# A decode row's share of a projection moved to four column groups of TensorE, and products of paged keys and queries moved from VectorE to GpSimd

## The reference, cut to what matters

```
h = rmsnorm(x)                                   # 1024 prompt rows, 8 sample rows, 1024 wide
sq, sk, sv, dq, dk, dv, ga, gb = split(h @ w_in) # first 3840 columns here, the gates later
dq, dk = rope(rmsnorm(dq)), rope(rmsnorm(dk))    # per head of 64
past = pool[page_table]                          # (8, 2048, 2, 8, 64), keys and values
z = einsum('bqhd,bkhd->bhqk', sq, past_keys) * 64 ** -0.5 + bias
```

## Time and profile before

| | us |
|---|---|
| median of 3 runs | 2374.56 |
| lowest, highest | 2369.94, 2378.31 |
| profiled execution | 2363.81 |
| its span, first to last instruction | 2362.0 |
| mean granted clock of TensorE | 0.949 of full speed |

### The profile page before, as it was taken

One profiled execution on the slowest core, in us unless ns is written; L12 is line 12 of the kernel. 1 busy time (PEld: TensorE's weight loads), 2 busy tenths in 40 slices (PEclk: granted clock), 3 DMA queues, 4 the chain that ended last, 5 costly groups with the idle time before them and its releaser, 6 DMA issues. The chain is left out here.

```text
span 2362.0 us, 38212 instructions
## 1 busy us (share of the span) xinstructions
PE 2154.9 (91%) x13126; PEld 1577.2 (67%) x13126; DVE 1416.2 (60%) x2146; ACT 1037.4 (44%) x1563; POOL 1022.6 (43%) x799
## 2 busy tenths in 40 slices
PE   7999799879699979999899979999999999999994
PEld 5777677667444438888777636776776677677663
DVE  4487678767576762111357527677667667766762
ACT  6221122245366652111234105666666566666662
POOL 2111222122366650011006603677677777767662
PEclk9999899957799999999999899999999999999997
DMA  6587701064445529893352059999999999999995
GB/s 219 171 271 246 225 32 38 28 190 124 161 135 155 169 82 299 263 302 112 110 190 91 23 194 319 332 323 318 326 329 318 323 329 321 323 325 326 319 320 136
DMA packets 180335, 520.57 MB, mean 220 GB/s; under 512 B 22908, under 2 KB 78867, under 8 KB 153791
## 3 DMA queue, kind: packets, MB, share of 16 engines
q1 hardware_dynamic: 133654, 366.37, 45.3%
q0 software_dynamic: 36208, 93.16, 15.6%
q10 hardware_dynamic: 10368, 59.73, 7.6%
HBM read 442.31 MB, written 125.08 MB: 240 GB/s over the span
## 5 line engine op out<-in xcount | busy, mean ns | idle before, releaser
L2474 DVE TENSOR_TENSOR w_gu_lo<-w_e,w_gu_hi 128x2048 fp32r<-128x2048 f32 x132 | 301.9, 2287 | 38.0 <-ACT w_gu_hi L2400 38.0
L2400 ACT ACTIVATE w_gu_hi<-w_e 128x2048 fp32r<-128x2048 f32 x132 | 253.5, 1920 | 44.4 <-DMA w_e<-in_w_e_gate 42.1
L565 PE MATMUL pP<-wring,hT_hi 128*128 128x512 f32 (+2 forms) x576 | 228.0, 396 | 21.8 <-DVE wring L500 12.7
L2336 PE MATMUL pG_e<-w_gu_hi,xT_hi 128*128 128x512 f32 x528 | 232.7, 441 | 1.0 <-issue 1.0
L567 PE MATMUL pP<-wring,hT_lo 128*128 128x512 f32 (+2 forms) x576 | 222.5, 386 | 0.0
L566 PE MATMUL pP<-wring,hT_hi 128*128 128x512 f32 (+2 forms) x576 | 222.3, 386 | 0.0
L2336 PE MATMUL pG_e<-w_gu_hi,xT_lo 128*128 128x512 f32 x528 | 208.9, 396 | 0.0
L2336 PE MATMUL pG_e<-w_gu_lo,xT_hi 128*128 128x512 f32 x528 | 208.1, 394 | 0.0
L2269 POOL DMA_INDIRECT x_scratch<-y_e,target x66 | 107.6, 1631 | 187.8 <-ACT y_tail L2438 187.8
L2255 POOL DMA_INDIRECT rows_tail<-h_scratch,index x66 | 176.5, 2675 | 20.8 <-issue 20.8
L429 ACT ACTIVATE stage<-pP 128x512 f32<-128x512 f32 (+3 forms) x72 | 41.1, 570 | 307.5 <-PE pP L567 303.5
(11 more groups left out here) (312 smaller groups left out, 5148.7 us busy)
## 6 DMA issues: line engine op xcount, KB each, us to landing
w_e<-in_w_e_gate SPq DMA_DIRECT2D x66, 1024.0 KB, 7.2
w_e<-in_w_e_up SPq DMA_DIRECT2D x66, 1024.0 KB, 11.5
w_e<-in_w_e_down SPq DMA_DIRECT2D x66, 1024.0 KB, 7.0
turned<-in_cache_sb_kv SPq DMA_DIRECT2D x256, 256.0 KB, 3.1
out<-in_cache_win_kv ACTq DMA_DIRECT2D x8, 4094.0 KB
turned<-in_w_in ACTq DMA_DIRECT2D x56, 256.0 KB, 6.2
turned<-in_w_in SPq DMA_DIRECT2D x16, 512.0 KB, 9.0
out<-in_cache_win_kv ACTq DMA_DIRECT2D x8, 1022.0 KB
```

The source lines that it names most:

```text
L565: pe.matmul(pP[:m, i % 4, :w], hi, w_hi(u), start=(c == 0), stop=False)
L2336: last = pe.matmul(pG[:, :, :], xs[:, r, c, :], ws[:, r, :, c, :], start=(n == 0), stop=(n == 3 * KC - 1))
L2400: act.activation(ghi[:, r, k, :, :].rearrange("p c f -> p (c f)"), w[:, r, k, :], ACT.Copy).then_inc(ghi_ready, 1)
L2474: dve.tensor_tensor(glo[:, r, k, :, :].rearrange("p c f -> p (c f)"), w[:, r, k, :], ghi[:, r, k, :, :].rearrange("p c f -> p (c f)").bitc ...
```

## The change

The first group keeps its order. In each later group the decode item comes first, at place 0, and the eight prompt tiles follow at places 1 to 8. For groups 1 to 7 the decode item is made in another way: eight float32 matmuls from the raw weights, not split, with the activations of the 8 decode rows padded to 32 columns with zeros. Chunk c goes to column group c % 4 of TensorE, that is to PSUM rows 32q to 32q + 31 (decode_parts). ScalarE copies these 128 rows to SBUF, and one more matmul with a 0/1 mask adds the four parts (decode_fold); TensorE issues it inside the next item, ahead of its third chunk. ScalarE's copy of the decode item waits for it in its place in the order. ScalarE also waits for decode_parts before it loads the next group's raw weights.

The products of keys and queries move from VectorE (score_keys) to GpSimd (weigh_keys), with their waits, at the same items; in GpSimd's program they stand behind the weight subtractions of place 8 and ahead of the item's square. VectorE keeps the reductions.

The additions to setup are three buffers, five semaphores, a zeroing on GpSimd, one copy on ScalarE of the decode rows' activations, and the mask, made by VectorE from the identity.

```diff
-        for t in range(NT):
+        for t in (range(NT) if not items else (NT - 1, *range(NT - 1))):
...
             def _(pool):
                 pool.memset(eps[:, :], EPS).then_inc(eps_set, 1)
+                pool.memset(hT_dec[:, :, :], 0.0).then_inc(dec_zero, 1)
...
+                def weigh_keys(n):
+                    s, c = divmod(n, NPC)
+                    if c == 0:
+                        pool.wait_ge(q_in[s % 2], 16 * (s // 2 + 1))
+                    pool.wait_ge(k_in[n % NKB], 16 * GP * (n // NKB + 1))
+                    if n:
+                        pool.wait_ge(s_score_ready, n)
+                    pool.tensor_tensor(prod, kbuf[:, n % NKB], q[:, s % 2, :].unsqueeze(1).broadcast_to([P, GP, SBW]),
+                                       ALU.mult).then_inc(s_prod_ready, 1)
...
                     if k < NK - 1 and t == NT - 1:
                         for c in range(POOL_LOW):
                             low_w((k + 1) * KC + c)
+                    if i in CHUNK_AT:
+                        weigh_keys(CHUNK_AT[i])
...
                     act.wait_ge(raw_ready, t + 1)
+                    if t == NT - 1:
+                        act.wait_ge(dec_zero, 1)
+                        act.activation(hT_dec[:, :, :NS], rawT(t), ACT.Copy).then_inc(dec_raw_ready, 1)
...
                         if t == 1:
+                            if k:
+                                act.wait_ge(dec_done, k)
                             for c in range(KC):
                                 load_w((k + 1) * KC + c)
...
                         m, w = rows_of(items[i]["t"]), items[i]["w"]
+                        if m == NS and k:
+                            act.wait_ge(dec_done, k)
+                            act.activation(dec_part[:, :w], pP[:, i % 4, :w], ACT.Copy).then_inc(dec_part_ready, 1)
                         act.wait_ge(p_ready, i + 1)
...
                 def score_keys(n):
                     s, c = divmod(n, NPC)
-                    if c == 0:
-                        dve.wait_ge(q_in[s % 2], 16 * (s // 2 + 1))
-                    dve.wait_ge(k_in[n % NKB], 16 * GP * (n // NKB + 1))
-                    if n:
-                        dve.wait_ge(s_score_ready, n)
-                    dve.tensor_tensor(prod, kbuf[:, n % NKB], q[:, s % 2, :].unsqueeze(1).broadcast_to([P, GP, SBW]),
-                                      ALU.mult).then_inc(s_prod_ready, 1)
                     dve.wait_ge(s_prod_ready, n + 1)
...
+                dve.wait_ge(ident_in, 16)
+                chain(dve.tensor_tensor(fold[:, :], ident[:, 0:NS], ident[:, 32:32 + NS], ALU.add))
+                chain(dve.tensor_tensor(fold[:, :], fold[:, :], ident[:, 64:64 + NS], ALU.add))
+                dve.tensor_tensor(fold[:, :], fold[:, :], ident[:, 96:96 + NS], ALU.add).then_inc(fold_ready, 1)
...
+                def decode_parts(i):
+
+                    k, w = i // NT, items[i]["w"]
+                    if k == 1:
+                        pe.wait_ge(dec_raw_ready, 1)
+                    pe.wait_ge(stage_ready, i - 3)
+                    for c in range(KC):
+                        q = c % QT
+                        pe.wait_ge(w_in[c], 16 * (k + 1))
+                        last = pe.matmul(pP[32 * q:32 * q + 32, i % 4, :w], hT_dec[:, c, :], w_raw(k * KC + c),
+                                         start=(c < QT), stop=(c >= KC - QT))
+                    last.then_inc(dec_done, 1)
+
+                def decode_fold(i):
+
+                    k, w = i // NT, items[i]["w"]
+                    if k == 1:
+                        pe.wait_ge(fold_ready, 1)
+                    pe.wait_ge(dec_part_ready, k)
+                    pe.matmul(pP[:NS, i % 4, :w], fold[:, :], dec_part[:, :w], start=True, stop=True).then_inc(p_ready, 1)
+
                 for i in range(NI + 2):
-                    if i < NI:
+                    if NT <= i < NI and i % NT == 0:
+                        decode_parts(i)
+                    elif i < NI:
...
                         for c in range(KC):
                             u = i // NT * KC + c
+                            if i > NT and i % NT == 1 and c == 2:
+                                decode_fold(i - 1)
...
-                            elif t == NT - 1:
+                            elif i % NT == NT - 1:
                                 last.then_inc(w_used, 1)
```

More of the change, by code:

```diff
@@ L166, in phase_project @@
         wraw = turned[:, 16:, :].rearrange("p a (b n) -> p (a b) n", n=512)
+        hT_dec = sb("hT_decode", [P, KC, P // QT])
+        dec_part = sb("decode_part", [P, 512])
+        fold = sb("decode_fold", [P, NS])
         stage = sb("stage", [P, NSTAGE, 512])
@@ L202, in phase_project @@
         p_ready = sem("p_ready")
+        dec_zero = sem("dec_zero")
+        dec_raw_ready = sem("dec_raw_ready")
+        dec_done = sem("dec_done")
+        dec_part_ready = sem("dec_part_ready")
+        fold_ready = sem("dec_fold_ready")
         stage_ready = sem("stage_ready")
@@ L349, in _ @@
                             low_w((k + 1) * KC + c)
+                    if i in CHUNK_AT:
+                        weigh_keys(CHUNK_AT[i])
                     if not items[i]["normed"]:
                         continue
-                    m = rows_of(t)
+                    m = rows_of(items[i]["t"])
                     pool.wait_ge(stage_ready, i + 1)
```

## The result

| | before | after |
|---|---|---|
| median, four runs each | 2373.05 | 2418.16 |
| lowest, highest | 2369.94, 2378.31 | 2416.91, 2428.60 |
| profiled execution's span | 2362.0 | 2415.3 |
| end of the projection in it | 473.5 | 520.1 |

The account below looks back on a forecast made before the run. The projection was taken as in balance: TensorE 6.0 us an item, VectorE's chunk 4.6, GpSimd mostly idle. Delay 45.5 plus 5.4 in groups 6 and 7 gave 51 us on a median of 2374.6: 2425, range 2392 to 2452.

Parts of the forecast that it names:

- product on GpSimd: One 128x2048 product of keys and queries, extrapolated from rows of smaller additions and a product: 4.5 us.
- end of product 31: Last GpSimd product in the projection, after 31 steps from a first product at 95.34: ends at 330.9.
- delay there: Lateness when group 5's decode item and one full item are done, 344.6 against 299.1 before: 45.5 us.
- The chain: Projection: GpSimd's product and VectorE's reduction take turns on one buffer, 7.0 us a chunk against 6.0 for TensorE's item.
- Rivals 1, 2 and 3: GpSimd product at 3.3 us (2387, chance 0.07), 5.7 (2464, 0.08), or below 2.9 (2362, 0.07).
- Rival 4: Decode matmuls' column groups don't overlap: 2 us more each item, 0 to 4 in all, 2427; inside the forecast's 0.78.
- The burst: GpSimd's five weight subtractions between two products at a group's end: 8.4 us, 5.6 at half width.
- The last item at the lower clock: Group 5's first full item: last four of eight chunks after the fifth subtraction at 1.2 GHz, 5.3 us.
- The decode item: Groups 1 to 7: 1.6 us where 5.6 stood, saving 4.0 in a full-width group, 2.0 in group 4.
- Rival 3: Product below 2.9 us, so the chain stays under TensorE and saved rows show: 13 us faster, 2362; chance 0.07.
- Groups 6 and 7: Short item under norm 7, norm 8's root held behind the fold: 62.5 against 59.8, +2.7 us at each boundary, 5.4.
- Neither is on the path: SyncE's key loads (keys 7.5 us after product n-2) and ScalarE's stage copies (slack of six items) are not late first.

Follow-up runs that it names:

- e2: Kernel before the change with only the products moved to GpSimd, decode rows as before: median 2423.1 us, ratio 1.0216 to the kernel before.
- e1: Changed kernel with the products of keys and queries back on VectorE, all else as changed: median 2370.8 us, ratio 0.9987 to the kernel before.
- e3: Changed kernel with each GpSimd product, and its reduction, made in two halves of 1024 elements: median 2403.8 us, ratio 1.0131 to the kernel before.
- e7: e1 with the fold issued ahead of norm 7's transposes in groups 6 and 7: median 2361.7 us, ratio 0.9966 to the kernel before.
- e6: e5 with all stores but the last of each prompt item in groups 3 and 4 issued by ScalarE: median 2356.3 us, ratio 0.9942.
- e5: e4 with group 6's weights loaded at place 2 of group 5, not place 1: median 2359.8 us, ratio 0.9962 to the kernel before.
- e4: Changed kernel with products on VectorE and the new decode form and order in groups 1 to 5 only: median 2360.1 us, ratio 0.9951.

## Why the prediction was right

Every step of its chain can be laid beside the rows. The mechanism came as forecast; the 4.4 us by which the forecast is too high at the projection's end are a sum of errors in both directions.

| step | forecast | measured |
|---|---|---|
| product on GpSimd | 4.5 | 4.58 (32 of them) |
| product to product | 7.0 | 7.1 |
| burst of subtractions | 8.4; 5.6 at half width | 7.54; 3.64 |
| end of product 31 | 330.9 | 329.6 |
| first full item of group 5 done | 344.6 | 340.6 |
| delay there | 45.5 | 41.5 |
| groups 6 and 7, excess over before | 2.7 each | 3.1 and 2.7 |
| end of the projection | 51 later | 46.6 later |
| median | 2425 | 2418.2 |

- **The chain** carried the argument, and the runs show it from both sides. With the products alone the loss is whole (e2), without them it is gone (e1), and with the turns broken up it shrinks to the next bound (e3). The extrapolation from rows of 256 to 768 elements to one of 2048 was right to 2%. Rivals 1, 2 and 3 fall with it: none of their prices for a product was met. Rival 4 falls too, by the decode item's row in e1: eight matmuls that did not overlap would take some 8 us at the fold's price, and took 1.92.
- **The burst** was too dear by 0.9 us each, by 2.0 at half width. The rows that I took had a product of VectorE take turns with each (3.42 us at 133.15 and 2.80 at 235.87, where it takes 2.29 alone). With the products away only VectorE's subtractions do, and at half width they began when the burst was nearly over (286.66, its end at 288.02). e1 has it the other way: with products on VectorE and the decode item short, the burst takes 10.4 us at 125.05. A duration from a contended row should have been cleaned of the contention that the change removes.
- **The last item at the lower clock** was too dear as well. I let four chunks of matmuls follow the last subtraction at half speed. TensorE had started on the first chunks at 330.94, right behind the first subtraction, and was back at full clock within the third chunk, so that the last four took 2.8 us and not 5.3. The four bursts were 4.5 us too dear in all and the end of the item behind the fifth subtraction 1.8, and the first product began 1.7 before 95.34. Against that, 32 products gave back 2.6 and the gaps between them 1.6. But for rounding that makes the 4.0 us by which the delay fell short: part of the closeness is luck, errors that cancel.
- **The decode item** was mis-sized: 2.9 us and not 1.6. I counted the records of the earlier trace rows as matmuls, and a float32 matmul leaves two. The item saves 2.7 us and not 4.0; over groups 1 to 5 that would be 12 us and not 18. That it did no harm to the forecast is luck of its place: in groups 2 to 5 it falls in the wait. Rival 3's price of 13 us was too good for the same reason, and would be 7.
- **Groups 6 and 7**: the root held behind the fold was expected 16.8 us after place 8's end and came at 16.3. e7 took the cause away and the time came back.
- **"Neither is on the path"** was true of SyncE and the key buffers only under a chain of 7 us, and even there not quite: the product at 303.97 waited 4.02 us for keys where a turn costs 2.46, because SyncE's issue stood behind a late item's stores, an order that the prediction named and then gave no price. Once the chain is gone they are next, at 6.5 us a chunk with GpSimd (e3), and with VectorE through the issues of SyncE (e6) and the weights that share the transfers (e5). That is one reason why e1 gave 6 us at the projection's end where 11 were expected; the decode item's size is the other. With 12 us from the item, less the 3.0 that e1 lost in groups 6 and 7, 9 us were to be had, and 3 are left for the keys, as far as one profile tells. My first expectation asked what TensorE saved and not what would then be last.

## What to carry to other kernels

An idle engine is not free capacity when its work and another engine's share one buffer: price the round trip (here 4.6 + 2.3 + 0.2 us against 6.0 of cover), and not the busy shares. A saving on the engine that sets the pace shows only up to the next limit, so follow the queue that feeds it, issue by issue, before counting the gain. And where an engine runs in order, a short item's copy that waits for a late one (the fold) holds everything written behind it.

## What the runs showed of the hardware

- Eight float32 matmuls of 32 by 512, over four column groups, took 1.92 us at full clock and 3.64 at the lower one; the fold of 8 by 512 took 1.02 and 1.87. Eight stand in the trace as 16 records and one as two.
- GpSimd's two-input float32 operations: 1024 elements 2.39 us, 2048 elements 4.58, also when VectorE's one-input sum ran beside them (e3). VectorE's two-input weight subtractions of 512 elements took 1.49 us in the mean in the changed kernel (11 of them, among GpSimd's products and bursts), where three in a row took 1.89 in all with GpSimd idle (e1, at 285.62). The Trainium skill, "SBUF — State Buffer", section "Who interferes with whom", tells of a port pair shared by the two engines and held exclusively, which VectorE does not need for an operation with one SBUF input outside its two-port modes, and does need for the second input of an operation with two; both observations agree with it.
- After a wait TensorE's return to the full clock varied for the same kind of gap: 2.7 us of slow matmuls after 4.34 us of idle time in the kernel before, 5 us in e4.
